# Low weight parts kept in the ring slot, four high buffers, and joint first tiles in a two-layer hybrid backbone

## The chip, the core and the metric

The kernel runs on one core of one Trainium2 chip. The metric is the device time of one execution in microseconds (us). TensorE (PE) multiplies, VectorE (DVE), ScalarE (ACT) and GpSimd (POOL) do the rest, and SyncE (SP) issues most of the DMAs.

## What is computed

The reference is a backbone of two layers over 512 latent and 256 context tokens, with 1024 channels, in float32. Each layer is a token mixer and an MLP, both behind an RMS norm with a modulation worked out from a conditioning vector:

```python
za, zb, zr, zd = jnp.split(h @ p['w_in'], IN_CUTS, axis=-1)
...                                   # four head groups: GQA, MLA, RWKV-7 scan, windowed GQA
y = merge_groups(outs) @ p['w_out']
yc = merge_groups(outs_c) @ p['w_out'] if with_ctx_out else None
...
return jnp.square(jax.nn.relu(h @ w1)) @ w2
```

`w_in` has about 2500 columns (20 tiles of 128 here), `w_out` 1024 (8 tiles), the MLP 4096 hidden units. In the second layer, which is the last, the context tokens are needed only as keys and values, so its queries, out-projection and MLP run over 512 tokens.

## The kernel before

**Tiles.** Activations lie transposed: 8 channel tiles k of 128 partitions by 768 tokens. A *tile* of a projection is 128 output channels: 8 channel tiles times spans of 512 and 256 tokens. To keep float32 accuracy with the faster float32r products, activations and weights are split into a high and a low part, and each term is three products (high weight x high, high weight x low, low weight x high): 48 matmuls per full tile, 24 in the last layer where it has 512 tokens. `part` inside `product` issues the three.

**The weight ring.** SP loads slabs of 512 KB (a tile's weights, 128x1024) into four slots of `slab`, tile n into slot n % 4. The split of a slab makes the high part `whi` (a cast to float32r) and the low part `wlo` (slab minus high). There are two buffers for each, by n % 2. POOL does both steps (`split`, lines 532 and 535); in the MLP ACT makes the high parts of all but the first two tiles of a round (line 986), which stand in ACT's order between its evictions. POOL's subtraction increments `s_used[q]`, which tells PE that the tile can start and SP that the slot can be loaded again. Before splitting tile n POOL waits on `s_tile` until PE has finished tile n-2. *Ring rows* (`ring_row`) are parts of the modulation weights: four raw slabs that PE multiplies straight out of the slots; PE increments `s_used` for them.

**Order.** Every engine has its order written out by hand. Per layer: in-projection (`w_in`, 20 tiles, the first 8 in a loop of two trips), attention and scan, out-projection (`w_out`, 8 tiles, the first two written out as `out_part`), MLP (a loop of 4 rounds; each has 8 tiles of `w1`, then 8 of `w2` that add into yT). Ring rows lie behind the in-projection (row 5 at once), behind the out-projection, and behind layer 0's MLP.

**First tiles.** Ahead of the in-projection and the MLP DVE makes the normed activations per channel tile: line 1064, then ACT's high part (line 693), then line 1071 for the low part. The first `product` of a stage gets `ready` and waits for k part by part; the others find everything there. In a round's second half the first tile waits for the hidden parts, which DVE makes from ACT's relu (line 990) in lines 1449 to 1451.

**Banks.** Tiles go in turn to PSUM columns 0 and 1024 (2048 and 3072 in the second half). ACT evicts (lines 730, 969 and 970, 990), DVE adds the second half's tiles (line 1456). PE waits on `s_ev` or `s_ev2` until the tile before last is evicted.

**DVE elsewhere.** In the out-projection's start DVE normalises the scan's output (lines 1307 to 1328) and makes low parts (line 1334). PE turns two of the results (line 2133) and finishes tiles 0 and 1 with them.

## Time and profile before

| | |
|---|---|
| median of 3 runs | 2366.45 us (2365.79 to 2367.32) |
| the profiled execution | 2361.28 us, its span 2359.5 us |
| busy: PE / DVE / POOL / ACT | 92% / 42% / 33% / 28% |
| mean granted clock of TensorE | 0.971 of 2.4 GHz |
| SP loads of weights | 128 of `w1`/`w2`, 40 of `w_in`, 16 of `w_out`, 96 of modulation, 512 KB each |

In a timeline row the first two numbers are the start and the duration in us. Rows are merged where instructions of one form follow each other ("x2"), and the bracket at the end is the engine's idle time before it and what ended it. The duration of a matmul includes its way through the pipeline, so matmuls follow each other more closely than they are long: read the distance between starts.

### The profile page before, as it was taken

The page shows a single profiled execution, that of the slowest core. Times are in us where ns is not written, and L with a number is a line of the kernel's source. Part 1 is how long each engine was busy: PE and PEld are TensorE (multiplying, and loading weights), DVE is VectorE, ACT ScalarE, POOL GpSimd, SP SyncE. Part 2 cuts the span into 40 slices and gives each one's busy share as a digit, 9 for nine tenths or more (in the row PEclk, how much of TensorE's full clock was granted, in tenths as well). Part 3 has the DMA queues.
Part 4 walks back from the last instruction along what each step waited for, and adds up shares of the span by engine and source line. Part 5 has one row for each costly group of instructions (what it writes and reads, how often), then busy time and mean ns, then how long its engine had stood idle before and what let it go on. Part 6 is the DMA issues. An engine that isn't in the chain of part 4 may idle for free.

```text
span 2359.5 us, 44992 instructions
## 1 busy us (share of the span) xinstructions
PE 2180.1 (92%) x19332; PEld 1771.2 (75%) x19332; DVE 996.8 (42%) x1506; ACT 666.7 (28%) x1166; POOL 771.2 (33%) x546
## 2 busy tenths in 40 slices
PE   5999899879988999999999799988879988999997
PEld 3888466659876788888888578846659965888885
DVE  3002366486644622314142510336576646442452
ACT  3110366642312211112021221146642223221221
POOL 3433333022142223232322243235204142444443
PEclk9999999989999999999999999999989999999998
DMA  6211100120022111111113231110030023222221
GB/s 264 92 58 54 72 1 1 60 73 4 13 81 90 63 63 63 62 62 62 62 62 133 98 114 54 36 72 1 17 115 3 4 90 121 94 98 98 90 96 62
DMA packets 45433, 162.85 MB, mean 69 GB/s; under 512 B 5504, under 2 KB 5504, under 8 KB 45024
## 3 DMA queue, kind: packets, MB, share of 16 engines
q1 hardware_dynamic: 44480, 157.89, 19.4%
q8 instruction: 124, 2.03, 0.3%
q0 software_dynamic: 800, 2.69, 0.3%
q14 instruction: 29, 0.24, 0.0%
HBM read 158.46 MB, written 2.10 MB: 68 GB/s over the span
## 4 chain that ended last, share of the span: by engine, by line
PE 81%; DVE 12%; ACT 4%; issue 2%; DMA 1%; POOL 0%; SPq 0%; POOLq 0%; ACTq 0%; DVEq 0%
PE ps L1465 77%; PE ps L1782 3%; DVE part_h L1071 1%; DVE hT L1064 1%; DVE small L1168 1%; DVE xT L1089 1%; DVE flat L1087 1%; ACT flat L781 1%; DMA flat<-wmod_dram 1%; DVE ps L1166 1%; DVE part_h L1334 0%; PE ps L2051 0%; DVE flat L1449 0%; DVE flat L1262 0%; DVE flat L1314 0%
## 5 line engine op out<-in xcount | busy, mean ns | idle before, releaser
L1465 PE MATMUL ps<-part_hi,wparts 128*128 128x512 f32 (+1 forms) x3072 | 825.3, 355 | 22.1 <-DVE part_h L1071 9.3
L1465 PEld LDWEIGHTS ps<-part_hi,wparts 128*128 128x128 f32 x3072 | 548.6, 191 | 113.9 <-DVE part_h L1071 12.5
L535 POOL TENSOR_TENSOR wparts<-flat,wparts 128x1024 fp32r<-128x1024 f32 x184 | 446.1, 2425 | 526.0 <-ACT wparts L986 520.2
L1465 PE MATMUL ps<-part_h,wparts 128*128 128x512 f32 (+1 forms) x1536 | 545.1, 355 | 0.0
L1465 PE MATMUL ps<-flat 64*64 64x32 f32 (+8 forms) x8200 | 429.8, 257 | 22.0 <-DVE flat L1279 13.1
L1465 PE MATMUL ps<-part_mlp,wparts 128*128 128x512 f32 (+1 forms) x1536 | 415.9, 358 | 14.1 <-DVE part_h L1071 8.3
L1465 PEld LDWEIGHTS ps<-flat 64*64 64x64 f32 (+4 forms) x8200 | 333.3, 142 | 104.9 <-issue 69.2
L1465 PEld LDWEIGHTS ps<-part_h,wparts 128*128 128x128 f32 x1536 | 296.2, 193 | 39.9 <-issue 1.4
L1465 PEld LDWEIGHTS ps<-part_mlp,wparts 128*128 128x128 f32 x1536 | 275.8, 191 | 57.9 <-POOL wparts L535 10.1
L986 ACT ACTIVATE wparts<-flat 128x1024 fp32r<-128x1024 f32 x112 | 118.8, 1061 | 696.3 <-PE ps L1465 696.3
L1465 PE MATMUL ps<-part_lo,wparts 128*128 128x512 f32 (+1 forms) x768 | 272.2, 354 | 0.0
L1449 DVE TENSOR_TENSOR flat<-flat 128x768 f32<-128x768 f32 (+1 forms) x64 | 158.6, 2479 | 212.1 <-ACT flat L990 211.6
L532 POOL CAST wparts<-flat 128x1024 fp32r<-128x1024 f32 x72 | 77.4, 1075 | 511.8 <-PE ps L1465 196.5
L1456 DVE TENSOR_TENSOR flat<-flat,ps 128x768 f32<-128x768 f32 (+1 forms) x64 | 52.5, 821 | 353.7 <-PE ps L1465 353.7
L1465 PEld LDWEIGHTS ps<-part_lo,wparts 128*128 128x128 f32 x768 | 145.2, 189 | 20.0
L1782 PE MATMUL ps<-kf,flat 128*128 128x128 f32 x592 | 91.3, 285 | 38.3 <-DVE hT L1183 17.6
L730 ACT ACTIVATE flat<-ps 128x768 f32<-128x768 f32 (+1 forms) x40 | 30.7, 769 | 308.4 <-PE ps L1465 308.4
L1782 PEld LDWEIGHTS ps<-kf,flat 128*128 128x128 f32 x592 | 65.5, 143 | 64.6 <-issue 32.9
L1168 DVE TENSOR_REDUCE small<-ps 128x1 f32<-128x768 f32 (+2 forms) x120 | 95.5, 812 | 31.9 <-PE ps L1465 30.5
L781 ACT ACTIVATE flat<-ps,small 128x768 f32<-128x768 f32 (+2 forms) x120 | 93.8, 785 | 47.3 <-DVE small L1168 29.8
L1131 DVE RECIPROCAL small<-small 128x48 f32<-128x48 f32 x2 | 0.9, 453 | 207.8 <-ACT small L736 207.8
L1465 PE MATMUL ps<-flat,silu 128*32 128x512 f32 x352 | 53.5, 715 | 29.8 <-DMA flat<-wmod_dram 28.3
(206 smaller groups left out, 2014.0 us busy)
## 6 DMA issues: line engine op xcount, KB each, us to landing
flat<-w_dram SPq DMA_DIRECT2D x128, 512.0 KB, 3.4
flat<-wmod_dram SPq DMA_DIRECT2D x88, 512.0 KB, 5.3
flat<-win_dram SPq DMA_DIRECT2D x40, 512.0 KB, 3.5
flat<-wout_dram SPq DMA_DIRECT2D x16, 512.0 KB, 3.6
hT<-wmod_dram SPq DMA_DIRECT2D x8, 512.0 KB, 7.5
xT<-xT_dram SPq DMA_DIRECT2D x8, 384.0 KB, 6.2
flat<-rope_dram SPq DMA_DIRECT2D x2, 1024.0 KB, 5.5
out_dram<-xT SPq DMA_DIRECT2D x8, 256.0 KB, 2.0
```

What stands on the lines that cost most here:

```text
L532: ch.link(pool.tensor_copy(whi[q % 2], src))
L535: pool.tensor_tensor(wlo[q % 2], src, whi[q % 2], ALU.subtract).then_inc(s_used[q], 1)
L730: nc_.activation(zv[:, tile, 0:t], ps[:, (q % 2) * 1024:(q % 2) * 1024 + t], ACT.Copy).then_inc(s_ev, 1)
L781: nc_.activation(prob[:, h % 2, 0:w], ps[:, (h % 2) * 1024:(h % 2) * 1024 + w], ACT.Exp, bias=small[:, h:h + 1], accum_out=small[:, 16 + h ...
L986: nc_.activation(whi[q % 2], slab[:, q * SLAB:(q + 1) * SLAB], ACT.Copy).then_inc(s_whi, 1)
L1064: ins = V.scalar_tensor_tensor(out=hv[:, k, a:b], in0=xv[:, k, a:b], scalar=gains[:, l, which, k, s:s + 1], in1=rs[:, a:b], op0=ALU.mult, ...
L1071: ins = V.scalar_tensor_tensor(out=pre_lo[:, k - 1, a:b], in0=hv[:, k - 1, a:b], scalar=mods[:, l, 12 * which + k - 1, s:s + 1], in1=pre_h ...
L1168: ins = V.tensor_reduce(nm, src, AX.X, ALU.max, negate=True)
L1449: ch.link(V.tensor_tensor(raw, raw, raw, ALU.mult))
L1456: V.tensor_tensor(yT[:, k, 0:t], yT[:, k, 0:t], ps[:, o:o + t], ALU.add).then_inc(s_ev2, 1)
L1465: return pe.matmul(out, lhsT, rhs, start=start, stop=stop)
L1782: ins = pe.transpose(ps[:, c:c + P], prob[:, h % 2, k * P:(k + 1) * P], ident)
```

## The change

Three things, in one diff.

- The low part is written back over the slab in its ring slot (`wlo[q]` is a float32r view of the slot), and `whi` has four buffers, one per slot, in the place of the two and two. A slot is then in use until PE has finished its tile: SP, and all who count rows, wait on `s_tile`, which ring rows increment too; `s_used` only tells PE that a split is done. POOL and ACT no longer wait for PE before they split: that a slab is loaded implies that its slot and its high buffer are free.
- `product` takes several tiles. With `ready` it goes channel tile by channel tile and does all its tiles for each. It waits for the splits of all of them first. In-projection: the first two tiles (layer 0) or three (last layer, the third in columns 512 to 1023, `in_bank`). MLP: the first two of each round's first half; of the second half the first alone (layer 0) or the first two (last layer).
- The loop over the first 8 in-projection tiles is written out. Its wait at the start of a trip, for all tiles before, becomes the usual wait for the tile before last.

ACT's cast in the MLP now stands ahead of its wait for the tile that it evicts next.

```diff
-        whi = [wparts[:, q * SLAB:(q + 1) * SLAB] for q in range(2)]
-        wlo = [wparts[:, (2 + q) * SLAB:(3 + q) * SLAB] for q in range(2)]
+        wrest = parts("wrest", "zT", F_SLAB, 4 * SLAB)
+        whi = [wparts[:, q * SLAB:(q + 1) * SLAB] for q in range(SLOTS)]
+        wlo = [wrest[:, q * SLAB:(q + 1) * SLAB] for q in range(SLOTS)]
...
+        def in_bank(l, n):
+            return 512 if l == LAST and n == 2 else n % 2 * 1024
...
-                        sp.wait_ge(s_used[q], 1 + used[0] + i)
+                        sp.wait_ge(s_tile[q], 1 + used[0] + i)
...
-                    pool.wait_ge(s_tile[(q - 2) % SLOTS], tile + (2 if q >= 2 else 1))
                     pool.sem_inc(s_sawslab, 1)
-                    ch.link(pool.tensor_copy(whi[q % 2], src))
+                    ch.link(pool.tensor_copy(whi[q], src))
                 else:
                     pool.wait_ge(s_whi, hi_done)
-                pool.tensor_tensor(wlo[q % 2], src, whi[q % 2], ALU.subtract).then_inc(s_used[q], 1)
+                pool.tensor_tensor(wlo[q], src, whi[q], ALU.subtract).then_inc(s_used[q], 1)
...
-                        act.wait_ge(s_tile[k % SLOTS], 1 + i * 4 + (TILES * l + T_MLP + k // SLOTS + 1))
-                        nc_.activation(whi[q % 2], slab[:, q * SLAB:(q + 1) * SLAB], ACT.Copy).then_inc(s_whi, 1)
+                        nc_.activation(whi[q], slab[:, q * SLAB:(q + 1) * SLAB], ACT.Copy).then_inc(s_whi, 1)
                         if k < KT:
+                            act.wait_ge(s_tile[k % SLOTS], 1 + i * 4 + (F_MLP[l] + k // SLOTS + 1))
...
+            def product(hi, lo, t, ready, *tiles):
...
+                for o, q, fill in tiles:
+                    pe.wait_ge(s_used[q], fill + (2 - rows[0]))
                 if ready is None:
-                    for a, b in spans:
-                        for k in range(KT):
-                            ins = part(k, a, b)
+                    for o, q, fill in tiles:
+                        for a, b in spans:
+                            for k in range(KT):
+                                ins = part(o, q, k, a, b)
+                        ins.then_inc(s_tile[q], 1)
                 else:
                     for k in range(KT):
                         pe.wait_ge(ready[0], ready[1] + k)
-                        for a, b in spans:
-                            ins = part(k, a, b)
-                return ins
+                        for o, q, fill in tiles:
+                            for a, b in spans:
+                                ins = part(o, q, k, a, b)
+                            if k == KT - 1:
+                                ins.then_inc(s_tile[q], 1)
...
                         if j and ring:
-                            ins.then_inc(s_used[q], 1)
+                            ins.then_inc(s_tile[q], 1)
...
+                first = 2 if l < LAST else 3
+                pe.wait_ge(s_ev, 1 + 60 * l)
+                product(pre_hi[0], pre_lo, t, (s_hlo, 16 * l + 1), *((in_bank(l, n), n, fills[0]) for n in range(first)))
+                for n in range(first, QUERY):
+                    win_tile(n, t)
...
+                    pe.wait_ge(s_ev, 1 + i * KT + (60 * l + NZ + KT))
+                    product(pre_hi[2], pre_lo, t, (s_hlo, 16 * l + 9), *((k * 1024, k, i * 4 + fills[0]) for k in range(2)))
...
+                    first = 1 if l < LAST else 2
+                    pe.wait_ge(s_ev2, 1 + i * KT + 32 * l)
+                    product(h1_hi, h1_lo, t, (s_h1, i * KT + (32 * l + 2)),
+                            *((2048 + k * 1024, k, i * 4 + (fills[0] + 2)) for k in range(first)))
```

## Rows read from the trace of the kernel before

**Rows 1.** The page: busy times (part 1) and the chain by engine (part 4).
```profile
PE 2180.1 (92%) x19332; PEld 1771.2 (75%) x19332; DVE 996.8 (42%) x1506; ACT 666.7 (28%) x1166; POOL 771.2 (33%) x546
...
PE 81%; DVE 12%; ACT 4%; issue 2%; DMA 1%; POOL 0%; SPq 0%; POOLq 0%; ACTq 0%; DVEq 0%
```

**Rows 2.** Timeline of ACT: two successive evictions, layer 0, then the last layer.
```profile
71.19 0.81 ACT L730 ACTIVATE flat<-ps 128x768 f32<-128x768 f32 x1 [6.61 <-PE ps L1465]
...
79.53 0.81 ACT L730 ACTIVATE flat<-ps 128x768 f32<-128x768 f32 x1 [6.65 <-PE ps L1465]
...
1374.62 0.60 ACT L730 ACTIVATE flat<-ps 128x512 f32<-128x512 f32 x1 [3.94 <-PE ps L1465]
...
1380.06 0.60 ACT L730 ACTIVATE flat<-ps 128x512 f32<-128x512 f32 x1 [3.96 <-PE ps L1465]
```

**Rows 3.** Timelines of PE and DVE, in-projection of layer 0.
```profile
49.66 0.50 PE L1465 MATMUL ps<-part_hi,wparts 128*128 128x512 f32 x1 [0.72 <-DVE part_h L1071]
...
88.91 0.47 PE L1465 MATMUL ps<-part_hi,wparts 128*128 128x512 f32 x1 [1.09 <-ACT flat L730]
...
59.00 2.42 DVE L1071 SCALAR_TENSOR_TENSOR part_h<-hT,modT,part_hi 128x512 fp32r<-128x512 f32 x4
```

**Rows 4.** Timelines of POOL, DVE and PE, out-projections of both layers.
```profile
654.35 2.72 POOL L535 TENSOR_TENSOR wparts<-flat,wparts 128x1024 fp32r<-128x1024 f32 x1
...
654.86 2.76 DVE L1314 TENSOR_TENSOR flat<-flat 128x512 f32<-128x512 f32 x1
...
662.57 0.69 DVE L1314 TENSOR_TENSOR flat<-flat 128x512 f32<-128x512 f32 x1
...
682.03 0.47 PE L1465 MATMUL ps<-part_hi,wparts 128*128 128x512 f32 x1 [1.33 <-POOL wparts L535]
...
1925.86 0.47 PE L1465 MATMUL ps<-part_hi,wparts 128*128 128x512 f32 x1 [1.54 <-POOL wparts L535]
```

**Rows 5.** Timelines of POOL, DVE and PE, MLP start of layer 0.
```profile
766.93 2.36 POOL L535 TENSOR_TENSOR wparts<-flat,wparts 128x1024 fp32r<-128x1024 f32 x1
...
766.93 3.31 DVE L1071 SCALAR_TENSOR_TENSOR part_h<-hT,modT,part_mlp 128x512 fp32r<-128x512 f32 x2
...
766.10 0.77 PE L1465 MATMUL ps<-part_mlp,wparts 128*128 128x512 f32 x1 [3.97 <-DVE part_h L1071]
...
789.83 0.50 PE L1465 MATMUL ps<-part_mlp,wparts 128*128 128x512 f32 x2
```

**Rows 6.** Stretches: length, five engines' busy times, granted clock, DMA share, GB/s.
```profile
758.00:793.00 35.00, 25.99 (x126) 21.94 (x126) 30.21 (x48) 11.44 (x20) 9.63 (x5) 0.80 0.30 106
1352.00:1380.00 28.00, 22.61 (x73) 15.51 (x74) 15.61 (x30) 11.44 (x20) 6.85 (x4) 0.76 0.12 39
```

**Rows 7.** Timelines of PE and POOL, MLP start of the last layer.
```profile
1986.15 0.79 PE L1465 MATMUL ps<-part_mlp,wparts 128*128 128x512 f32 x1 [5.74 <-POOL wparts L535]
...
1989.71 0.63 PE L1465 MATMUL ps<-part_mlp,wparts 128*128 128x512 f32 x2
...
1987.62 2.71 POOL L535 TENSOR_TENSOR wparts<-flat,wparts 128x1024 fp32r<-128x1024 f32 x1
```

**Rows 8.** PE at the end of layer 0's MLP; a ring row's single DMA: KB, us to landing.
```profile
1310.51 1.92 PE L1465 MATMUL ps<-flat,silu 128*32 128x512 f32 x16
1312.37 2.84 PE L1465 MATMUL ps<-kf,flat 128*128 128x1 f32 x24
...
flat<-wmod_dram SPq DMA_DIRECT2D x1, 512.0 KB, 3.4
```

**Rows 9.** Timeline of POOL: the last split before PE starts layer 1's in-projection.
```profile
1348.03 2.38 POOL L535 TENSOR_TENSOR wparts<-flat,wparts 128x1024 fp32r<-128x1024 f32 x1
```

**Rows 10.** Timelines around a second half's start in the last layer.
```profile
2037.64 0.50 PE L1465 MATMUL ps<-part_hi,wparts 128*128 128x512 f32 x1 [0.67 <-DVE part_lo L1451]
...
2033.28 0.58 ACT L990 ACTIVATE flat<-ps 128x512 f32<-128x512 f32 x1
...
2038.64 0.69 DVE L1456 TENSOR_TENSOR flat<-flat,ps 128x512 f32<-128x512 f32 x1 [1.05 <-PE ps L1465]
```

More of the change, by code:

```diff
@@ L522, in _, with split @@
                 pool.sem_inc(first, 1)
-            def split(q, fill, tile, hi_done=None):
+            def split(q, fill, hi_done=None):
                 src = slab[:, q * SLAB:(q + 1) * SLAB]
@@ L528, in split, with splits @@
                     pool.wait_ge(s_slab[q], (fill + 1) * 16)
-                    pool.wait_ge(s_tile[(q - 2) % SLOTS], tile + (2 if q >= 2 else 1))
                     pool.sem_inc(s_sawslab, 1)
-                    ch.link(pool.tensor_copy(whi[q % 2], src))
+                    ch.link(pool.tensor_copy(whi[q], src))
                 else:
                     pool.wait_ge(s_whi, hi_done)
-                pool.tensor_tensor(wlo[q % 2], src, whi[q % 2], ALU.subtract).then_inc(s_used[q], 1)
-            def splits(n, per, fill, tile, hi=None):
+                pool.tensor_tensor(wlo[q], src, whi[q], ALU.subtract).then_inc(s_used[q], 1)
+            def splits(n, per, fill, hi=None):
                 with pool.Fori(0, n) as i:
@@ L545, in splits @@
                             done = None if hi is None or k < 2 else i * (2 * KT - 2) + (hi + k - 1)
-                            split(q, i * per + (fill + j), i * per + (tile + j), done)
+                            split(q, i * per + (fill + j), done)
                     ch.leave(n)
@@ L562, in _ @@
                     sum_squares(0, 0)
-                splits(NZ // SLOTS, 1, F_IN[l], TILES * l)
+                splits(NZ // SLOTS, 1, F_IN[l])
                 pool.memset(vD[:, 0, :], 0.0)
@@ L651, in _ @@
                     pool.wait_ge(s_y[x], answered(l, STEPS))
[L652 to L653 removed]
+                splits(KT // SLOTS, 1, F_OUT[l])
+                splits(FFG, 4, F_MLP[l], FFG * (2 * KT - 2) * l)
                 sum_squares(l, 3)
@@ L728, in _ @@
                         act.wait_ge(s_pss, l + 1)
-                    act.wait_ge(s_tile[q], 1 + n // SLOTS + (TILES * l + 1))
-                    nc_.activation(zv[:, tile, 0:t], ps[:, (q % 2) * 1024:(q % 2) * 1024 + t], ACT.Copy).then_inc(s_ev, 1)
+                    act.wait_ge(s_tile[q], 1 + n // SLOTS + (F_IN[l] + 1))
+                    o = in_bank(l, n)
+                    nc_.activation(zv[:, tile, 0:t], ps[:, o:o + t], ACT.Copy).then_inc(s_ev, 1)
                     if tile in NORMED:
@@ L1465, in mm, with part @@
                 return pe.matmul(out, lhsT, rhs, start=start, stop=stop)
-            fills = [0]
-            def product(hi, lo, o, q, fill, t, ready=None):
-                pe.wait_ge(s_used[q], fill + 2)
+            fills, rows = [0], [0]
+            def product(hi, lo, t, ready, *tiles):
                 spans = ((0, LAT), (LAT, TOK)) if t == TOK else ((0, LAT),)
-                def part(k, a, b):
+                def part(o, q, k, a, b):
                     out = ps[:, o + a:o + b]
-                    w1, w2 = (w[q % 2][:, k * P:(k + 1) * P] for w in (whi, wlo))
+                    w1, w2 = (w[q][:, k * P:(k + 1) * P] for w in (whi, wlo))
                     mm(out, w1, hi[:, k, a:b], k == 0, False)
@@ L1557, in ring_row @@
                 fills[0] += 1
+                rows[0] += 1
             def early_row(n):
@@ L1599, in _, with win_tile @@
                     keep_clock(0, 3)
-                for first, last, cols in ((0, QUERY, t),):
-                    with pe.Fori(first // SLOTS, last // SLOTS) as i:
-                        for q in range(SLOTS):
-                            tile = i * SLOTS + (60 * l + q)
-                            if l or q >= 2:
-                                pe.wait_ge(s_ev, 1 + tile - 1)
-                            else:
-                                pe.wait_ge(s_ev, 1 + i * SLOTS)
-                            ins = product(pre_hi[0], pre_lo, (q % 2) * 1024, q, i + fills[0], cols,
-                                          (s_hlo, 16 * l + 1) if q == 0 else None)
-                            ins.then_inc(s_tile[q], 1)
-                def win_tile(n):
-                    q = n % SLOTS
-                    pe.wait_ge(s_ev, 1 + 60 * l + n - 1)
-                    product(pre_hi[0], pre_lo, (q % 2) * 1024, q, n // SLOTS + fills[0], TOK).then_inc(s_tile[q], 1)
+                def win_tile(n, cols=TOK):
+                    pe.wait_ge(s_ev, 1 + 60 * l + max(n - 1, 0))
+                    product(pre_hi[0], pre_lo, cols, None, (in_bank(l, n), n % SLOTS, n // SLOTS + fills[0]))
+                first = 2 if l < LAST else 3
[3 more added lines that the diff above has]
+                    win_tile(n, t)
                 def head_sums(n):
@@ L2123, in _ @@
                 for n in range(2):
-                    pe.wait_ge(s_used[n], fills[0] + 2)
+                    pe.wait_ge(s_used[n], fills[0] + (2 - rows[0]))
                     if n:
```

54 lines of the change are left out of this document (23 added, 31 removed).

## The prediction

> **What bounds the kernel now.** I read the page first, for who ends last. TensorE (PE) is busy 92% of the span and carries 81% of the chain of waits, VectorE (DVE) 12%, ScalarE (ACT) 4% [rows 1]. So for most of the time the span is a row of matrix tiles, and only what makes PE wait can be won. Next I went through PE's own timeline for every place where it stands still beside a projection tile. The steady tiles have none: ACT starts one eviction of 768 columns at 71.19 and the next at 79.53, so a full tile takes 8.34 us, and in the last layer, with 512 columns, 5.44 us (1374.62 to 1380.06) [rows 2]. There are 64 full tiles in layer 0's MLP and no gap of 0.2 us between them. What can be won or lost stands at the edges of the stages: the starts of the in-projections (about 47 and 1352), of the out-projections (640 to 683, 1890 to 1926) and of the MLPs (758 to 793, 1980 to 2000), the end of layer 0's MLP (1310), and four small gaps in the middle of the last layer's MLP rounds.
>
> **What the change does at a start.** Today the first tile follows the channel tiles k as DVE finishes them: PE waits 0.72 us, then 0.8 us, before each [rows 3]. One k costs a full tile 8.34/8 = 1.04 us and DVE 2.11 us, so half of that time is lost. With two tiles per k (2.08 us), or three of 512 columns in the last layer (3 x 0.68 = 2.04 us), the wait is filled with work that is needed anyway. Set against this are four prices, which I take from rows.
>
> First, DVE against GpSimd (POOL). A split is a cast of 1.04 us and a subtraction of about 2.4 us on POOL. Where a DVE operation with two SBUF inputs meets one, it waits: 0.69 us become 2.76 us beside the subtraction that began at 654.35, and a pair that takes 1.15 us becomes 3.31 us beside the one at 766.93 [rows 4, 5]. The operation of line 1064, which reads PSUM for one input, keeps its 0.73 us. Today POOL may split two tiles and must then wait for PE. With four high buffers it splits four at once, so two more splits (7 us of POOL) fall on DVE's chain at four stage starts, two of them in the out-projections, where DVE is the chain.
> The Trainium skill, "SBUF — State Buffer", section "SBUF: two separate sides", says that the port pair which the two engines share is an exclusive lock held for a whole instruction, and counts a DVE operation with two SBUF inputs among those that need it. The trace agrees (0.69 us against 2.76). By that rule the two added splits aren't free wherever DVE ends last; without it I would leave 6.5 us out of the sum.
>
> Second, the clock. After a wait TensorE runs at 1.2 GHz instead of 2.4: the clock over 758 to 793 was 0.80, over 1352 to 1380 0.76 [rows 6]. At the MLP start of the last layer the first three products from 1986.15 are 0.42 us apart and from 1989.7 0.23 us [rows 7]: 3.5 us at half rate, 1.7 us lost. A single tile hides this in its waits for DVE; joint tiles have no waits left, so each pays it.
> The Trainium skill, "TensorE: Matmul & The Clock Gate", section "The HAM clock gate", has idling throttle the array and activity release it. The rows show the same order here, and it speaks against starting later with more work.
>
> Third, a joint start waits for the weights of all its tiles. Fourth, a ring slot is now free when PE has finished its tile, not when POOL has split it.
>
> **The sum, place by place** (minus is faster).
>
> Layer 0 in-projection: the last k is ready at 61.4 [rows 3]. The two more splits, from 43.5 to 50.6, cover the first two low-part operations of DVE (46.34, 48.46) and move the rest by about 2.5 us: 63.9, plus 2.08 us of both tiles, 66.0; half of the price of a slow clock, 0.8 us: 66.8. Today the second tile ends at 71.0: -4.2. The loop's edge disappears too: the fifth tile waits today until the fourth is evicted (1.09 us) [rows 3], the new code asks for the third: -1.2.
>
> Ring row after the in-projection, both layers: its last slab is now fetched from the end of the last tile, 246.4; a single 512 KB load lands after 3.4 us [rows 8], so 249.9 to 250.0 where the row starts today at 249.67: +0.3 each, +0.6.
>
> Layer 0 out-projection: the four POOL operations from 649.19 to 657.07 cost DVE about 5 us today: four of its operations are longer than their like elsewhere, by 0.8, 1.3, 0.8 and 2.1 us (the last 2.76 for 0.69) [rows 4]. Four more follow at once, and from 658 to 671 DVE has nothing but such operations, at whose end PE starts again: +5.0. In return the third tile no longer waits for its split, 1.33 us and the tail of a product: -1.5. Together +3.5. Layer 1 has the same with 4.7 and 1.54 us [rows 4]: +3.0.
>
> Layer 0 MLP start: the second split ends at 769.3, so the joint start is at 769.35, not 766.10 [rows 5]. ACT hands out no third split before 780.9, so DVE is as today. 2 x 8.34 = 16.7 us of work plus 2.2 us for 4.3 us at half rate: 788.3. Today the eight last spans of the second tile start at 789.83 and it ends at 792.7 [rows 5]: -4.3.
>
> Layer 0 MLP end: PE goes straight from the last tile into the ring row at 1310.51 and from there into the sums at 1312.37, which is the chain [rows 8]. The row's fourth slab can now be asked for only at 1310.5 and lands after 3.4 us: +3.5, and 0.5 for the clock after an idle stretch of that length: +4.0.
>
> Layer 1 in-projection: today the third tile ends at 1379.8 (its eviction starts at 1380.06) [rows 2]. POOL, free at 1350.4 [rows 9], splits two more until about 1358: the first k is late by up to 2 us (1356.1). From there 3 x 5.44 = 16.3 us and 2.1 us for the clock: 1374.5, and about 0.8 us more because the fourth tile needs the second's bank, whose eviction stands behind an eviction and a square of ACT (0.60 and 0.84 us): 1375.3 against 1379.8, -4.5.
>
> Layer 1 MLP start: DVE is quick here (one segment). PE starts at 1986.15, today as soon as the first split is done; the second is done at 1987.62 + 2.71 = 1990.33 [rows 7]. So 1990.4 + 10.9 + 1.7 + 0.2 = 2003.2; today two tiles end at 1999.5: +3.7.
>
> Layer 1 MLP rounds: today each second half waits 0.67 us (0.83 with the tail of a product) for the last hidden part [rows 10]; two joint tiles cover 9.5 us and end that. But tiles that end 0.68 us apart leave no time to evict: DVE's addition (0.69 us) starts 0.46 us after the first tile's last product and frees its bank 1.20 us after it, PE wants it after 0.91: +0.29. ACT's eviction in the first half (0.58 us) likewise +0.24. Four times (0.83 - 0.29 - 0.24): -1.2. In layer 0 the same sum leaves 0.13 us four times: +0.5. Its second half still starts with one tile, and covers 7.3 us where DVE needs 6.
>
> Everything else I set at nothing. A reload has three tiles (16.3 us in the last layer) for a load of 3.4 us and a split of 3.5 us; if ACT's casts came a tile later, this would cost about 1 us a tile. The addresses of the low parts change no duration that a row shows.
>
> Sum: -4.2 -1.2 +0.6 +3.5 +3.0 -4.3 +4.0 -4.5 +3.7 -1.2 +0.5 = -0.1 us. The profiled execution took 2361.28 us (span 2359.5), 5.2 us under the median of the runs; I carry the difference over: 2366.45 - 0.1 = 2366.3 us.
>
> **The rivals.** (a) The added splits don't hold DVE up, because POOL comes to them later or finds DVE between waits. Then both out-projections gain 1.5 us instead of losing 3, and the two in-projections gain 2 us more each: about -13, 2353 us. Against it: from 657 on nothing keeps POOL, since slabs three and four of the out-projection were asked for by 650. (b) No clock penalty at the joint starts, as PE is busy in them without gaps: four times about 1.7 us, -7, 2359 us. For it: in layer 0's in-projection PE comes warm from filler products. (c) Slower: the clock. PE now stands idle 7 to 10 us ahead of both MLP starts and 5 us longer in both out-projections; if half rate lasts 8 us rather than 4 in the joint starts and in the rows behind 1310, four places lose 2 us each: +8, 2374 us. It decides from about 6 us at half rate. (d) Slower still: the ring of four is too shallow in the last layer because ACT's casts stand behind its evictions; 1 us in some twenty tiles, 2385 us. (e) The change fails to do what it says at a start because the weights come later than the k parts. That is the MLP of layer 1 already, and in the sum.
>
> **How the numbers follow.** Forecast 50%, (a) 14%, (b) 15%, (c) 16%, (d) 5%. The likeliest case's own range is 2361 to 2371, from +-2 us on each DVE and clock term. To hold 8 in 10 the range takes in (b) and (c): 2356 to 2374. A measurement of this kernel tells about 0.2% (4.7 us) from no change. Faster by more than that: (a), (b) and a tenth of the rest, 0.30; slower: (c), (d) and a little, 0.24; within 0.46.
>
> **What would show it.** Right: PE without waits on DVE in the in-projection starts; PE idle 3.5 us before the row at 1310; DVE operations near 2.8 us between 657 and 665; the first product of the last MLP about 4 us later after its last ring row; no wait on the last hidden part there. Wrong: any of the four prices absent, above all POOL's third and fourth splits outside DVE's chains, or a wait of PE for POOL inside the last layer's rounds.

## The result

Over four runs beside four of the kernel before, the changed kernel takes 2401.93 us (2400.08 to 2406.42) where the kernel before takes 2366.12 us (2362.92 to 2367.32): a ratio of 1.016, 95% interval 1.0145 to 1.0175. I had forecast 2366.3 us, within 2356 to 2374. The forecast was wrong by 36 us, in the direction of slower.

The page of the changed kernel, parts 1, 3 and 4, as far as they answer to [rows 1]:

```profile
PE 2193.9 (91%) x19332; PEld 1785.3 (74%) x19332; DVE 1039.0 (43%) x1506; ACT 667.5 (28%) x1166; POOL 790.2 (33%) x546
...
q8 instruction: 153, 2.51, 0.4%
...
PE 83%; DVE 9%; ACT 3%; issue 3%; DMA 1%; POOL 0%; SPq 0%; DVEq 0%; ACTq 0%; POOLq 0%
```

VectorE (DVE) went from 12% to 9% of the chain, as it should if the joint starts fill its waits. But TensorE (PE) is busy 14 us longer for the same 19332 products, and "issue", time in which an engine waited for nothing that the profile shows, is 3% instead of 2%. The queue that carries instructions (q8) moved 153 packets (124 before). I had not read that line, and most of what the change lost shows in it.

I cut each trace at the first and the last product that reads weights from the split buffers. These are the lengths of the stages in us (L0 and L1 are the two layers; a second trace of both kernels, from the last experiment, shows what differs between two executions of one program):

| stage | before | before again | after | after again |
|---|---|---|---|---|
| start of the L0 in-projection | 47.6 | 48.3 | 52.0 | 52.1 |
| L0 in-projection | 198.8 | 196.8 | 192.7 | 192.7 |
| middle of L0 | 407.0 | 412.1 | 408.8 | 413.8 |
| L0 out-projection | 78.9 | 77.7 | 80.1 | 82.1 |
| to the MLP's first product | 33.8 | 33.9 | 38.6 | 38.6 |
| L0 MLP | 544.5 | 544.5 | 562.0 | 564.5 |
| L0 MLP's end to the L1 in-projection | 43.5 | 43.5 | 56.2 | 53.5 |
| L1 in-projection | 175.4 | 175.3 | 169.1 | 169.1 |
| middle of L1 | 374.9 | 374.5 | 378.5 | 378.8 |
| L1 out-projection | 54.3 | 57.7 | 59.7 | 59.6 |
| to the MLP's first product | 27.4 | 27.8 | 30.4 | 30.5 |
| L1 MLP | 354.5 | 354.5 | 353.9 | 353.8 |

The L0 MLP stands out. Behind its first tile, which waits for DVE, the kernel before has no gap over 0.2 us in it; PE's timeline of the changed kernel has three, each at the edge between two rounds of the loop (first column: start; in brackets: the idle time before it and what ended it). Behind each the clock is at half its rate (second fence: length, five engines' busy times, then the granted clock):

```profile
913.81 0.77 PE L1468 MATMUL ps<-part_mlp,wparts 128*128 128x512 f32 x1 [5.54 <-issue]
```

```profile
913.80:916.30 2.50, 2.49 (x8) 2.12 (x8) 0.00 (x0) 0.00 (x0) 0.00 (x0) 0.50 0.03 7
930.00:1040.00 110.00, 110.00 (x632) 97.05 (x631) 42.17 (x30) 19.40 (x21) 42.27 (x17) 1.00 0.21 67
```

The other two are at 1054.79 (5.62 us) and 1197.29 (6.07 us). In the gap itself (908.3 to 913.8) ACT and POOL do nothing and DVE has 0.95 us of work, and from 913.8 to 916.3 all three do nothing: nobody was behind. Stretches of 5, 10 and 10 us behind the gaps have a granted clock of 0.71, 0.74 and 0.70, so half rate lasted 2.9, 5.2 and 6.0 us. The gaps (17.2 us) and half of that time (7.1 us) make 24.3 us, about the 23 us by which this stage is longer than where the gaps are gone (e1_shift64, below).

### The profile page after: what moved, and what is told of

It is laid out like the page before. It is cut to its first block, busy times and chain, and to the rows that moved or that the text cites. A ratio compares the mean times of both kernels' runs of the same rounds, so it can differ in the third digit from the quotient of the medians.

```text
span 2400.7 us, 44828 instructions
## 1 busy us (share of the span) xinstructions
PE 2193.9 (91%) x19332; PEld 1785.3 (74%) x19332; DVE 1039.0 (43%) x1506; ACT 667.5 (28%) x1166; POOL 790.2 (33%) x546
## 4 chain that ended last, share of the span: by engine, by line
PE 83%; DVE 9%; ACT 3%; issue 3%; DMA 1%; POOL 0%; SPq 0%; DVEq 0%; ACTq 0%; POOLq 0%
PE ps L1468 79%; PE ps L1777 3%; DVE small L1171 1%; DMA flat<-wmod_dram 1%; DVE xT L1092 1%; DVE flat L1090 1%; ACT flat L784 1%; DVE ps L1169 1%; DVE part_h L1337 1%; PE ps L2046 0%; DVE flat L1317 0%; DVE part_h L1074 0%; PE ps L1931 0%; DVE flat L1261 0%; DVE flat L1265 0%
## 5 line engine op out<-in xcount | busy, mean ns | idle before, releaser
L537 POOL TENSOR_TENSOR wrest<-flat,wparts 128x1024 fp32r<-128x1024 f32 x184 | 463.6, 2521 | 509.8 <-ACT wparts L988 503.8
L1468 PE MATMUL ps<-part_hi,wparts 128*128 128x512 f32 (+1 forms) x1536 | 547.8, 357 | 19.1 <-DVE part_h L1337 9.2
L1468 PE MATMUL ps<-part_hi,wrest 128*128 128x512 f32 (+1 forms) x1536 | 541.7, 353 | 0.0
L1468 PEld LDWEIGHTS ps<-part_hi,wparts 128*128 128x128 f32 x1536 | 294.4, 192 | 66.2 <-DVE part_h L1337 11.4
L1468 PEld LDWEIGHTS ps<-part_hi,wrest 128*128 128x128 f32 x1536 | 293.8, 191 | 39.6
L1468 PE MATMUL ps<-part_mlp,wparts 128*128 128x512 f32 (+1 forms) x768 | 278.4, 362 | 33.6 <-issue 17.2
L1468 PE MATMUL ps<-part_mlp,wrest 128*128 128x512 f32 (+1 forms) x768 | 275.6, 359 | 0.0
L1468 PEld LDWEIGHTS ps<-part_mlp,wparts 128*128 128x128 f32 x768 | 148.4, 193 | 57.9 <-issue 34.1
L1468 PEld LDWEIGHTS ps<-part_mlp,wrest 128*128 128x128 f32 x768 | 148.2, 193 | 21.5
L1454 DVE TENSOR_TENSOR part_lo<-flat,part_hi 128x768 fp32r<-128x768 f32 (+1 forms) x64 | 156.5, 2445 | 2.2
```

The source lines that it names most:

```text
L537: pool.tensor_tensor(wlo[q], src, whi[q], ALU.subtract).then_inc(s_used[q], 1)
L1454: V.tensor_tensor(h1_lo[:, k, 0:t], raw, h1_hi[:, k, 0:t], ALU.subtract).then_inc(s_h1, 1)
L1468: return pe.matmul(out, lhsT, rhs, start=start, stop=stop)
```

## The experiments

**Whose gap is it? Theory 1, instruction fetch; theory 2, a wait of the joint start.** The instruction queue (q8) of the changed kernel over 930 to 1300, rounds two to four of that loop:

```profile
q8 instruction: 22, 0.36, 0.4%
```

The kernel before has no such line in this stretch. In the first round both fetch alike, one 16 KB packet about every 22 us; the kernel before brings its last at 892.7 of a loop that runs from 766.1 and none in the later rounds, the changed kernel one at 903.3 and then, at the edge, at 907.0, 911.4 and 914.9, about 4 us apart. Laid over the order of the built program (a weight load and a multiplication for each pass, one place for everything else), the six transfers of the first round in the kernel before, at 783.5 to 892.7, span 1281 places: five blocks of 256. Counted so, the loop's body is 1572 places in the kernel before and 1570 in the changed one, hardly over six blocks of 256. In the kernel before it lies from place 70 of a block to place 106, in the changed one from 194 to 228. The expectations below say that it touches one block less in the one position than in the other. That is miscounted: it lies in seven blocks in both. What differs is how far it gets in the seventh. Counting the products between the transfers of the first round, in all traces a block's transfer starts between its places 146 and 191 (a few places uncertain, as some records are missing), or at once where the loop begins beyond them. A body that ends at 106 never comes to that point of its seventh block, one that ends at 228 does in every round. Two runs put the body elsewhere without changing any work.

```diff
             pe.wait_ge(s_silu, 3)
-            pe.wait_ge(s_const, 48)
+            for _ in range(128 + 1):
+                pe.wait_ge(s_const, 48)
```

> The changed kernel with 64 more instructions on TensorE's queue at its very start (128 waits that are already met, two to an instruction), ahead of a transfer that TensorE waits for until 19 us: they cost no time, and every later instruction of TensorE stands 64 places further on. Theory 1: the gaps of 5.5, 5.6 and 6.1 us at the three round edges of layer 0's MLP (913.81, 1054.79, 1197.29 in the changed kernel) are fetches of instructions. Counted in the built program (a weight load and a multiplication for each pass, one for every other instruction), the loop's body is 1570 instructions; in the kernel before it starts at place 70 of a block of 256 and ends at 106, in the changed kernel at 194 and 228. In the traces a 16 KB instruction transfer comes every 22 us or so in the first round; later rounds have none in the kernel before, and about nine each in the changed kernel, the three at an edge 4 us apart (907, 911, 914.5). The body then touches one block more than TensorE keeps; 64 places on it starts at place 2, ends at 36 and touches one block less. The gaps go, with the half-speed stretch behind each: about 20 us, 2382 us, and so do the instruction transfers of the later rounds. Theory 2: the gap is a wait of the joint start (banks, splits or parts) that the profile doesn't name; places don't matter: 2402 us, three gaps.

Measured: 2381.59 us (2378.9 to 2384.0), ratio 1.0071 (1.0044 to 1.0099) to the kernel before, 20.3 us under the changed kernel. The loop takes 539.0 us instead of 562.0, without a gap at a round's edge, and of instruction queues only this is left over 930 to 1300 (it is not q8):

```profile
q14 instruction: 1, 0.01, 0.0%
```

The converse, the same edit with 248 in the kernel before:

> The kernel before with 124 more instructions at the same point (248 met waits), so that the body of layer 0's MLP starts at place 194 of a 256-instruction block and ends at 230, where the changed kernel's stands at 194 and 228. Nothing else differs. Theory 1 (instruction fetch at the round's edge): three gaps of 5.5 to 6 us appear in a loop that had none over 0.2 us, with instruction transfers in every round: about 2386 us, 20 us over the kernel before. Theory 2 (the joint start's own waits): no gap, 2366 us.

Measured: 2390.64 us (2387.28 to 2395.17), ratio 1.011 (1.008 to 1.0139). The loop takes 562.7 us instead of 544.5, and the gaps are there, in a kernel without joint starts; q8 over 930 to 1300 moved 22 packets, as in the changed kernel:

```profile
915.81 0.76 PE L1465 MATMUL ps<-part_mlp,wparts 128*128 128x512 f32 x1 [4.97 <-issue]
```

The other two are 4.54 and 4.76 us. Theory 2 falls: the gap goes with the place and not with the joint start. With the body at places 2 to 36 (38 in e3_mlp_single), 30 to 64, 70 to 106 or 86 to 122 of a block no run has it, with 194 to 228 or 230 every run has it. That each transfer brings a block ahead of its use, and that the one started in the body's seventh block is one more than PE keeps and pushes out the loop's head, fits all of this and is an inference. If PE keeps eight blocks, the transfer must bring the block after the next one; if it keeps seven, the next. No run tells the two apart, and a body of another length (by more than 2) wasn't run.
The Trainium skill, "Advanced Engine Details and Errata", section "ISA Cache", gives TensorE 128 KB in lines of 16 KB, 256 instructions, which is eight; the packet size and the 256 places agree. The Trainium skill, "Runtime: NRT & Kernel Launch", section "Instruction fetch mechanics", says that a taken branch whose target is outside "the current 2-page window" stalls for a fetch. The trace of before speaks against that window for this engine: it jumps back 1572 instructions three times with no gap over 0.2 us and no transfer. The Trainium skill, "Advanced Engine Details and Errata", section "ISA Cache", also has "Only 2 cache lines!", and the same three jumps speak against that for TensorE.

**What does the joint start of the MLP give?** The edit for the first half of a round, on top of e1_shift64; the second half starts with `first = 1` in both layers, so that no round has a joint start.

```diff
-                    pe.wait_ge(s_ev, 1 + i * KT + (60 * l + NZ + KT))
-                    product(pre_hi[2], pre_lo, t, (s_hlo, 16 * l + 9), *((k * 1024, k, i * 4 + fills[0]) for k in range(2)))
-                    for k in range(2, KT):
+                    for k in range(KT):
                         pe.wait_ge(s_ev, 1 + i * KT + (60 * l + NZ + KT + k - 1))
-                        product(pre_hi[2], pre_lo, t, None,
+                        product(pre_hi[2], pre_lo, t, (s_hlo, 16 * l + 9) if k == 0 else None,
```

> As the first of these (the changed kernel, 64 places on), and in the MLP of both layers every round starts with one tile alone, as in the kernel before, in both halves; the ring, the splits and the joint starts of the input products stay. Against the first of these it tells what the joint start of the MLP costs or gives. Theory 1 (a joint start waits for the second split, 771.98 in layer 0, and in the last layer 8.77 us for POOL's wrest, and gives nothing back): 3 to 4 us less in layer 0 and about 3 in the last, less the 4 edges of 0.67 us that come back in each of the last layer's rounds, so some 4 us below the first of these, about 2378 us. Theory 2 (the joint start pays, since the channel tiles come one by one): 3 us or more above it.

Measured: 2380.68 us (2370.11 to 2384.36), not to be told from e1_shift64. The stages say why. In layer 0, from the out-projection's end to the MLP's end, 580.2 us against 576.0 in e1_shift64: the joint start gives 4.2 us. In layer 1 379.6 against 384.2: there it costs 4.6. I had only the second half of this right; the two cancel. In layer 1 PE waits for the second split [rows 7] and has little of DVE's to fill (the changed kernel):

```profile
2028.01 0.76 PE L1468 MATMUL ps<-part_mlp,wparts 128*128 128x512 f32 x1 [8.77 <-POOL wrest L537]
```

**The end of layer 0's MLP.** The stretch to the next in-projection grew by 12.7 us, of which 9.2 lie before the first sums of the updated stream (before 1310.6 to 1320.66, after 1334.1 to 1353.42). PE's timeline of the changed kernel, to be read beside [rows 8]:

```profile
1337.88 3.64 PE L1468 MATMUL ps<-flat,silu 128*32 128x512 f32 x16 [3.77 <-DMA flat<-wmod_dram]
1341.45 5.28 PE L1468 MATMUL ps<-kf,flat 128*128 128x1 f32 x24
1347.38 2.93 PE L1468 MATMUL ps<-kf,small 128*128 128x128 f32 x12 [0.65 <-DVE small L1042]
```

The wait is the one I had forecast (3.77 us). But in this trace all three groups behind it run at half rate: 3.64 for 1.92, 5.28 for 2.84, 2.93 for 1.70 us (the same stretch, with its clock third from the end, 0.50):

```profile
1337.90:1350.30 12.40, 11.75 (x52) 8.46 (x52) 0.19 (x1) 0.75 (x2) 0.00 (x0) 0.50 0.46 169
```

It isn't always so. The second trace of the changed kernel has the same wait (3.74 us), then 3.34, 2.84 and 2.93 us: the sums ran at full rate, and the stretch is 2.7 us shorter. The line of the sums there:

```profile
1350.79 2.84 PE L1468 MATMUL ps<-kf,flat 128*128 128x1 f32 x24
```

Of the six traces with this order and this wait four have the sums at 5.28 us and two at 2.84.

Two runs take the sums out from behind the row, each on top of e1_shift64.

```diff
+                sums(l, 3)
                 if l < LAST:
                     ring_row(0)
-                ssq(l, 3)
+                spread_root(l, 3)
```

> As the first of these, and behind layer 0's MLP the sums of squares for the norm stand ahead of the ring row instead of behind it, so that TensorE does them while the row's transfer is still under way (3.77 us at 1334 in the changed kernel), and the spread of the norm's root behind the row. Theory 1 (the ring row's late transfer, and the half speed that follows its gap, delay the norm's chain by row 3.64 + gap 3.77 and part of the sums' 5.28): the sums run at full speed in 2.84, the root is ready before the row is done, and the spread starts 5 to 7 us earlier: 2376 us where the first of these gives 2382. Theory 2 (the chain behind, with its waits for ACT and for the transfers of the early rows, sets the start of layer 1's input product whatever the norm does): within 1 us of the first.

Measured: 2376.04 us (2372.47 to 2378.91), 5.5 us under e1_shift64; the stretch is 49.8 us instead of 56.3. Then the row behind the spread as well:

```diff
+                ssq(l, 3)
                 if l < LAST:
                     ring_row(0)
-                ssq(l, 3)
```

> As e1_shift64, and behind layer 0's MLP both the sums of squares and the spread of the norm's root stand ahead of the ring row, whose products then fall into TensorE's wait for the first squares of the updated stream. In e4_sums_first, where the spread stands behind the row, the root was ready at 1320.6 and the spread started at 1323.5, and layer 1's in-projection started 49.7 us behind the end of the MLP, against 56.2 in e1_shift64 and 43.5 in the kernel before. Theory 1 (the row is off the chain once it stands behind the spread): another 2.5 to 3 us, so about 47 us behind the MLP's end and 9 us under e1_shift64: 2373 us. Theory 2 (the row then delays the tile sums behind it by as much): no more than e4_sums_first gave, 2376 us.

Measured: 2371.09 us (2364.71 to 2379.17), 10.5 us under e1_shift64; the stretch is 47.2 us. The row now fits between the spread and the first sums, at 2.78 us and with 1.60 us to spare:

```profile
1319.41 2.93 PE L1468 MATMUL ps<-kf,small 128*128 128x128 f32 x12 [0.65 <-DVE small L1042]
1322.27 2.78 PE L1468 MATMUL ps<-flat,silu 128*32 128x512 f32 x16
1326.65 2.85 PE L1468 MATMUL ps<-flat,kf 128*128 128x512 f32 x8 [1.60 <-ACT flat L682]
```

**Do the added splits hold DVE up?** On top of e1_shift64, POOL waits for DVE's last low part before the splits that the first product doesn't need (s_hlo in the in-projections, s_otl in the out-projections):

```diff
+            def first_splits(fill, early, done, value):
+                for q in range(SLOTS):
+                    if q == early:
+                        pool.wait_ge(done, value)
+                    split(q, fill)
...
-                splits(NZ // SLOTS, 1, F_IN[l])
+                first_splits(F_IN[l], 2 if l < LAST else 3, s_hlo, 16 * l + KT)
+                splits(NZ // SLOTS - 1, 1, F_IN[l] + 1)
...
-                splits(KT // SLOTS, 1, F_OUT[l])
+                first_splits(F_OUT[l], 2, s_otl, KT * (l + 1))
+                splits(KT // SLOTS - 1, 1, F_OUT[l] + 1)
```

> As e1_shift64, and of the first four splits of each in-projection and out-projection, POOL holds back those that the first product doesn't need (the third and fourth; in the last layer's in-projection the fourth alone) until DVE has made the last low part of that stage. Theory 1 (a POOL subtraction stretches the DVE operations that meet it, and a joint start turns that into a later start of TensorE): DVE's first low-part pair of the in-projection falls from 3.86 to about 1.15 us and TensorE starts 2.5 us earlier; each out-projection loses 4 to 5 us of its wait ahead of its seventh and eighth channel tiles, and the third tile doesn't wait for its split, since 4 us of products stand between; the last layer's in-projection gains 0 to 3: in all 9 to 13 us under e1_shift64, about 2371 us. Theory 2 (DVE is held up by something else, its two SBUF inputs or ACT's parts): DVE's durations stay and the held splits come late for tile 3: the same or some us above e1_shift64, 2382 to 2390 us.

Measured: 2362.35 us (2357.05 to 2366.23), 19.2 us under e1_shift64, ratio 0.9987 (0.9977 to 0.9996) to the kernel before. The in-projection starts at 48.6 instead of 52.0; the out-projections take 78.1 and 54.4 us (79.8 and 59.5), the stretch to the L1 in-projection 52.4 (56.3). That is 14 us; the rest lies in stages that the edit doesn't touch (the middle of L0 is 3.8 shorter, that of L1 4.0 longer, L0's in-projection 2.4 shorter) and in the median against the one profiled execution. DVE and POOL at three places of the changed kernel: the first low parts of the L0 in-projection, the out-projection, the L1 in-projection.

```profile
47.98 3.86 DVE L1074 SCALAR_TENSOR_TENSOR part_h<-hT,modT,part_hi 128x512 fp32r<-128x512 f32 x2
48.90 2.67 POOL L537 TENSOR_TENSOR wrest<-flat,wparts 128x1024 fp32r<-128x1024 f32 x1
...
658.44 3.98 DVE L1337 TENSOR_TENSOR part_h<-hT,part_hi 128x768 fp32r<-128x768 f32 x2
658.58 3.03 POOL L537 TENSOR_TENSOR wrest<-flat,wparts 128x1024 fp32r<-128x1024 f32 x1
...
1386.15 4.05 DVE L1074 SCALAR_TENSOR_TENSOR part_h<-hT,modT,part_hi 128x512 fp32r<-128x512 f32 x2
1387.26 2.66 POOL L537 TENSOR_TENSOR wrest<-flat,wparts 128x1024 fp32r<-128x1024 f32 x1
```

The first two of these DVE groups in e5_hold_splits, and POOL's first held split, which now starts when DVE is done:

```profile
47.30 1.15 DVE L1083 SCALAR_TENSOR_TENSOR part_h<-hT,modT,part_hi 128x512 fp32r<-128x512 f32 x2
...
655.02 1.82 DVE L1346 TENSOR_TENSOR part_h<-hT,part_hi 128x768 fp32r<-128x768 f32 x2
...
62.57 1.04 POOL L534 CAST wparts<-flat 128x1024 fp32r<-128x1024 f32 x1 [18.10 <-DVE part_h L1083]
```

3.86 became 1.15 and 3.98 became 1.82 us, for the same operations.
The exclusive lock that the Trainium skill describes ("SBUF — State Buffer", section "SBUF: two separate sides") would give just this, and the trace agrees with it.

**The clock at a joint start.** On top of e1_shift64:

```diff
+                pe.wait_ge(s_ev, 1 + 60 * l + NZ + KT)
+                keep_clock(0, 7 if l < LAST else 9)
                 with pe.Fori(0, FFG) as i:
```

> As e1_shift64, and ahead of the MLPs' first tiles TensorE runs filler products (7 in layer 0, 9 in the last, 0.88 us each) in the 7.2 and 8.8 us for which it waits for the second split. Theory 1 (half speed behind the wait is what idling costs, and the joint start pays it in full): the granted clock over the first 3 us, 0.50 in both, becomes 1.00, the products there stand 0.23 us apart instead of 0.45, and each MLP ends about 2 us earlier: 4 us under e1_shift64, 2378 us. Theory 2 (the products are slow for another reason, such as DVE's and POOL's traffic beside them, or the fillers outlast the wait): the products keep their 0.45 us or start later, 0 to +2 us.

Measured: 2373.2 us (2371.89 to 2375.49), 8.4 us under e1_shift64. The first 3 us of L0's MLP, first in e1_shift64, then in e6_fillers (columns as above: 9 products against 17, clock 0.50 against 1.00):

```profile
776.40:779.40 3.00, 2.93 (x9) 2.48 (x10) 3.00 (x7) 1.00 (x2) 0.00 (x0) 0.50 0.00 0
```

```profile
775.10:778.10 3.00, 3.00 (x17) 2.60 (x18) 3.00 (x7) 1.10 (x2) 0.00 (x0) 1.00 0.00 0
```

The MLPs are 3.4 and 2.3 us shorter (535.6 and 351.6), 5.7 in all where 4 was expected; the other 3 us lie in stages without fillers and in the median against the one profiled execution. I had taken 4.3 us of half rate for layer 0. In the changed kernel the clock over the first three stretches of 3 us from 772.1 is 0.50, 0.73 and 1.00, which makes 4.6 us and bears that out; in e1_shift64 the second stretch is still at 0.53, which makes 5.8.

**All together, and the kernel before mended likewise.**

The met waits and the held splits are those above; the fillers, the norm and the last layer's start:

```diff
+                pe.wait_ge(s_ev, 1 + 60 * l + NZ + KT)
+                keep_clock(0, 7 if l < LAST else 5)
+                together = 2 if l < LAST else 1
                 with pe.Fori(0, FFG) as i:
...
+                ssq(l, 3)
                 if l < LAST:
                     ring_row(0)
-                ssq(l, 3)
```

> The changed kernel with what the runs before pointed to, together: its later instructions 64 places on (and some 30 more by the fillers, so that the body of layer 0's MLP starts at place 30 and ends at 64), the splits that the first product doesn't need held back until DVE is done, filler products ahead of the MLPs, the norm ahead of the ring row, and in the last layer's MLP a single first tile. Added up by stages against e1_shift64 (2381.6 us): start of the first in-projection -3.4, first out-projection -1.7, layer 0's MLP -3.4, from its end to the next in-projection -9.1 by the norm and up to -3.9 by the held split, second out-projection -5.1, last MLP -4.6 by the single tile and about -1 by its fillers: -28 to -32, 2350 us. Theory 1 (each was a separate wait): 2345 to 2354 us, below the kernel before. Theory 2 (they overlap, one wait standing behind another, and the norm's gain is what the held split gives again): half of it, 2366 us.

Measured: 2346.1 us (2342.39 to 2347.63), ratio 0.9919 (0.9905 to 0.9932): 17.9 us under the kernel before. Against e1_shift64 the start is 3.2 us earlier, the out-projections 4.5 and 8.2 shorter, L0's MLP 3.4, the stretch to L1 12.0 (44.3 us, against 43.5 in the kernel before), L1's MLP with its start 4.5. The waits were separate, as theory 1 had it.

The same additions that make sense in the kernel before:

```diff
+                pe.wait_ge(s_ev, 1 + 60 * l + NZ + KT)
+                keep_clock(0, 4 if l < LAST else 6)
                 with pe.Fori(0, FFG) as i:
...
+                ssq(l, 3)
                 if l < LAST:
                     ring_row(0)
-                ssq(l, 3)
```

> The kernel before (two high and two low buffers, one tile at a time, nothing moved to another place but by the fillers, place 86 to 122 for the body of layer 0's MLP) with the norm ahead of the ring row and with fillers ahead of both MLPs (4 and 6). It tells what is left of the change itself once its own losses are mended: the row (1.9 us) leaves the chain at layer 0's end, and the fillers keep the clock where DVE sets the pace in layer 0 anyway, and give up to 1.5 us in the last layer. Theory 1 (joint starts are worth 6 us in each in-projection's length and 4 in layer 0's MLP, and e8_together keeps them): about 2362 us here, 10 us or more above e8_together. Theory 2 (the gains of e8_together come from the norm and the fillers alone and the joint starts give nothing): within 3 us of e8_together.

Measured: 2368.87 us (2362.39 to 2372.75), ratio 1.0015 (1.0004 to 1.0026). I had expected 2362; the additions give the kernel before nothing. The stretch is 43.6 us as without them, because the second half of the sums waits 0.69 us for ACT's last square and PE then runs at half rate there too. So what e8_together wins over the kernel before comes from the four buffers and the joint starts together, once they no longer pay for the rest; no run tells how much is due to each.

**How much do two executions of one program differ?**

> The kernel before, unchanged, for one more trace: how far do stages that nothing changes differ between two executions of one program? The two middle stages (from the last input-projection tile to the first output-projection tile) took 407.0 and 374.9 us in the first trace, 408.8 and 378.5 in the changed kernel, 410 to 417 and 375 to 381 in its variants. Theory 1 (the middle differs between executions by a few us, by the clock and by where the instruction blocks end): another trace of the same program gives values that differ from the first by 1 to 4 us. Theory 2 (the change costs the middle 5 us): 407 and 375 again within 1 us.

> The changed kernel, unchanged, for one more trace. The three gaps at the round edges of layer 0's MLP are a matter of the program's layout, not of the execution: again three, 5 to 6 us each, and 2400 to 2406 us. The middle stages: theory 1 (execution to execution) other than 408.8 and 378.5 by 1 to 4 us; theory 2 (a cost of the change) within 1 us.

Measured: 2367.08 and 2409.72 us (one run each), the stages as in the table above. The three gaps are there again (5.73, 5.88 and 5.88 us). The middle of L0 moves by 5 us between executions of one program, so its 1.7 us can't be called a cost of the change. Over all traces it takes 407.0 to 412.1 us (mean 409.4) in the four with the work of the kernel before, and 408.8 to 416.6 (mean 412.9) in the nine with that of the changed one: some 3.5 us may belong to the change, and why stays open. The middle of L1 doesn't move so (374.9 and 374.5; 378.5 and 378.8): its 4 us belong to the program. But e2_before_shift124, which has the same work as the kernel before, has 378.4 too, and e1_shift64, the changed kernel with nothing but its instructions moved, has 375.4. The "issue" gaps of over 0.3 us there add up to 3.8 us in the kernel before (4.9 in its second trace), 7.5 in e2_before_shift124, 5.3 in the changed kernel and 5.5 in e1_shift64. All 20 of them in the first trace of before and of after, in e1_shift64 and in e2_before_shift124 begin 0.2 to 2.0 us behind the start of a 16 KB instruction transfer, of which this stretch has 43 or 44 in some 375 us. So PE most likely waits for instructions there too, and the layout of the instructions can make or take the 4 us. That it is the whole reason isn't shown: e4_sums_first, with as many instructions as e1_shift64, has 378.2.

## Why the prediction was wrong

**"Everything else I set at nothing" and "no gap of 0.2 us between them": the step that failed.** I took the steady tiles of layer 0's MLP as fixed and asked only how their operands come. The loop of the in-projection, written out, was costed as one edge wait less (-1.2 us). That it also moves every later instruction, and so the body of a loop of 1570 instructions, was in no part of the sum and in no rival. Against e1_shift64's 539.0 us it makes this stage 23 and 25.5 us longer in the two traces; by the medians it is 20.3 us. This alone takes the time out of the range: 2366.3 plus 20 is 2386. What the runs showed in place of "nothing" is three gaps of 5.5 to 6.1 us at the rounds' edges and half rate for 2.9 to 6.0 us behind each, which go and come with the place of the body alone.

**End of layer 0's MLP, forecast +4.0, measured +9.2 and, in the second trace, +6.5.** The transfer was right (3.5 against 3.77 us). "0.5 for the clock" was the mis-sized term: half rate cost 5.4 us over the three groups (1.7, 2.4 and 1.2 us), in the second trace 2.7 over the first and the last. That is rival (c), whose mechanism I had (idle, then half rate for longer) and whose weight was too low. e4_sums_first and e7_norm_first give 6.5 and 9.1 us back.

**L0 in-projection, forecast -5.4, measured about -1.** DVE's stretch was right: 3.86 us for 1.15, 2.7 where I had 2.5. Two steps were wrong. The added splits begin to hold DVE up before the low parts: that pair starts at 47.98 instead of 46.34, 0.8 us of it because DVE's `gain` operation (line 1056, 1059 in the changed kernel) takes 0.93 instead of 0.17 us beside the third split; the sum had no term for that. And the sum counts from the last channel tile (63.9 plus 2.08). With the work of two tiles PE no longer waits for DVE at all: it starts at 51.99 instead of 47.64, then has 16.7 us of products, some of them at half rate (the clock is 0.72 and 0.71 over 52 to 54.5 and 54.5 to 58, which costs 1.7 us). That makes 70.4; the third tile's first product starts at 70.48, where I had 66.8. The third tile's eviction starts at 79.13, against 79.53 [rows 2]. The loop's edge gave 1.4 us as forecast (1.2).

**L1 in-projection, forecast -4.5.** The stage is 6.3 us shorter, but its start is 3.5 us later by the splits (a DVE pair of 4.05 us; the wait before it is 6.32 us, 2.91 before), where I had allowed "up to 2": -2.8.

**Out-projections, forecast +3.5 and +3.0.** Over two traces each +2.8 (81.1 against 78.3) and +3.6 (59.65 against 56.0). Right, and for the reason given: e5_hold_splits removes it. The second is less sure than it looks, as the two traces of the kernel before have 54.3 and 57.7 there.

**MLP starts and rounds, forecast -3.8 and +2.5.** Layer 1 with its start: 384.3 against 382.1, +2.2, right. Layer 0 without its gaps (e1_shift64) 576.0 against 578.3, -2.3: the joint start's worth of 4 us was right against e3_mlp_single; PE's own start came at 772.08 instead of 769.35, since the out-projection ended 1.2 us later and the norm's spread behind it ran at half rate (2.93 us from 736.93, where the kernel before has 1.63).

**The rivals.** (a) fell: the splits do hold DVE. (b) fell: over the first 3 us the clock was 0.50 at both MLP starts and at the start of the last layer's in-projection; e6_fillers is what makes (b) true. (c) was right and too light. (d) fell: no wait for a cast in the rounds of the last layer. (e) was in the sum for layer 1 only; in layer 0 PE waits 7.24 us for POOL's second split as well. Without the gaps the changed kernel is at 2381.6, still 7.6 us over the range's end and 15.3 over the forecast. By stages, the trace of e1_shift64 against the mean of the two traces of the kernel before: the end of layer 0's MLP and the L1 in-projection take 7.1 us more than forecast, the middle of layer 0, which was set at nothing, 7.0 (416.6 against 409.6, of which 5 is the spread between two executions), the first in-projection 2.6 and layer 0's MLP with its start 1.5.

## What to carry to other kernels

When an edit makes the program longer or shorter ahead of a long loop, ask where in its blocks of 256 the loop's body now begins and ends, and whether the engine still keeps all of it: look at the instruction queue in the traces of both versions, round by round, and shift the loop by a few dozen cheap instructions before judging the edit. A wait that a change adds costs its own length and can cost half rate behind it, on everything that follows in the chain (here 2.7 to 5.4 us behind a wait of 3.8); look for work that can stand in the wait, the chain's own first of all. And a buffer that lets an engine work ahead also lets it collide: hold the early work back with one semaphore until the critical engine is done.

## What I had not expected of the hardware

- A loop of 1570 instructions on TensorE ran without any instruction transfer after its first round at some places in the program, and at others stood still for 4.5 to 6.1 us at each round's edge, with four 16 KB transfers about 4 us apart, and ran at half clock behind it (2.9, 5.2 and 6.0 us in the changed kernel). The body lay in seven blocks of 256 either way; those that ended at place 36 to 122 of the seventh had no gap, those that ended at 228 or 230 had it.
- Behind an idle stretch of 3.77 us the clock stood at 0.50 for 12.4 us (1337.9 to 1350.3), in which TensorE was busy for 11.75 with small products; in the second execution of the same program, behind 3.74 us, it was back for the second of the three groups (2.84 us for the 24 sums) and at 0.50 again for the third. Behind 7.24 us of idling ahead of layer 0's MLP it was back at 1.00 after 4.6 us of tile products, in e1_shift64 after 5.8. Seven filler products in that wait (e6_fillers) kept it at 1.00 from the first tile product on.
- Stages in which nothing was changed differ by up to 5.1 us between two executions of one program (407.0 and 412.1), and by 3.5 us between programs that do the same work at other places.
